# Second block of tokens 0-255 woven with the expert gather of tokens 256-511

## What is computed

```python
def expert_block(args):              # per block of 128 tokens
    hb, eb, gb = args
    a = jax.nn.gelu(jnp.einsum('td,ted->te', hb, u_tab[eb]).astype(jnp.float32), approximate=False)
    w = (gb * a).astype(hb.dtype)
    return jnp.einsum('te,ted->td', w, v_tab[eb])
...
mask = k_chunk[None, :] <= (q_pos // CHUNK)[:, None]
...
```

## Time and profile before

| | us |
|---|---|
| median of 3 runs | 2968.13 (2965.42 to 2969.78) |
| the profiled execution | 2965.35 |
| its span in the profile | 2963.6 |
| first layer and scores, to the start of `stage_peer` | 0 to 677.6 |
| `stage_peer` | 677.6 to 2052.6 |
| half a | 2052.6 to 2467.6 |
| half b | 2467.6 to 2963.6 |

### The profile page before, as it was taken

One profiled execution on the slowest core, in us unless ns is written; L12 is line 12 of the kernel. 1 busy time (PEld: TensorE's weight loads), 2 busy tenths in 40 slices (PEclk: granted clock), 3 DMA queues, 4 the chain that ended last, 5 costly groups with the idle time before them and its releaser, 6 DMA issues. The chain is left out here.

```text
span 2963.6 us, 22217 instructions
## 1 busy us (share of the span) xinstructions
PE 2303.9 (78%) x7379; PEld 1329.2 (45%) x7379; DVE 1289.2 (44%) x2945; ACT 744.4 (25%) x1626; POOL 1071.8 (36%) x746
## 2 busy tenths in 40 slices
PE   4896698681677777777786877776967997778899
PEld 1345343571233333333332333332746885556787
DVE  1107541317667666775668555554252102243101
ACT  1202231211111111111111111112444444344443
POOL 1000000220434444444443444442704885400687
PEclk8897698895898999989998999987958998866999
DMA  6100151323999999999999999995603664300465
GB/s 214 51 14 0 57 171 57 94 74 127 420 420 420 409 420 420 420 385 419 421 419 416 398 420 420 420 420 230 212 0 99 186 185 141 107 1 8 144 185 161
DMA packets 172295, 710.32 MB, mean 240 GB/s; under 512 B 18033, under 2 KB 70812, under 8 KB 106140
## 3 DMA queue, kind: packets, MB, share of 16 engines
q0 software_dynamic: 73728, 536.90, 43.8%
q1 hardware_dynamic: 90576, 168.18, 18.0%
q10 hardware_dynamic: 7886, 3.93, 0.5%
HBM read 699.24 MB, written 9.72 MB: 239 GB/s over the span
## 5 line engine op out<-in xcount | busy, mean ns | idle before, releaser
L1382 PE MATMUL ps<-uv_ring,expert_diag 128*128 128x512 f32 x2048 | 1008.1, 650 | 340.4 <-ACT expert_diag L1351 340.3
L1187 POOL DMA_INDIRECT uv_ring<-in_peer_uv_dram,expert_idx x512 | 556.2, 1086 | 821.5 <-PE ps L1382 712.5
L1306 DVE CUSTOM_DVE_ANT_0 uv_ring<-uv_ring,h_rows 128x1024 f32<-128x1024 f32 x512 | 628.9, 1230 | 492.0 <-DMA uv_ring<-in_peer_uv_dram,expert_idx 491.4
L1382 PEld LDWEIGHTS ps<-uv_ring,expert_diag 128*128 128x128 f32 x2048 | 414.4, 208 | 933.5 <-issue 500.3
L1464 POOL TENSOR_TENSOR w_low_b<-w_raw_b,w_high_b 128x1024 fp32r<-128x1024 f32 x98 | 234.4, 2394 | 262.6 <-ACT w_high_b L1458 261.2
L1351 ACT ACTIVATE expert_diag<-ident,expert_weight 128x128 f32<-128x128 f32 x512 | 163.6, 390 | 623.5 <-DVE expert_weight L1278 623.5
L1464 POOL TENSOR_TENSOR w_low_a<-w_raw_a,w_high_a 128x1024 fp32r<-128x1024 f32 x98 | 235.2, 2403 | 199.4 <-ACT w_high_a L1458 198.1
L271 POOL TENSOR_TENSOR peerq_low<-peerq_raw,peerq_high 128x1024 fp32r<-128x1024 f32 x16 | 38.1, 2381 | 550.6 <-ACT peerq_high L260 550.6
L1344 ACT ACTIVATE expert_gelu<-expert_dot 128x4 f32<-128x4 f32 x128 | 26.3, 205 | 495.7 <-DVE expert_dot L1306 495.7
L1458 ACT CAST w_high_b<-w_raw_b 128x1024 fp32r<-128x1024 f32 x98 | 102.9, 1053 | 116.8 <-PE ps L1477 116.8
L1458 ACT CAST w_high_a<-w_raw_a 128x1024 fp32r<-128x1024 f32 x98 | 102.9, 1052 | 115.4 <-PE ps L1477 115.4
(11 more groups left out here) (399 smaller groups left out, 2896.2 us busy)
## 6 DMA issues: line engine op xcount, KB each, us to landing
w_raw_a<-in_w_gu_dram SPq DMA_DIRECT2D x44, 512.0 KB, 3.5
w_raw_b<-in_w_gu_dram SPq DMA_DIRECT2D x44, 512.0 KB, 3.6
wada_rest<-in_w_ada_dram SPq DMA_DIRECT2D x16, 1024.0 KB, 5.3
w_raw_a<-in_w_in_dram SPq DMA_DIRECT2D x24, 512.0 KB, 4.4
w_raw_b<-in_w_in_dram SPq DMA_DIRECT2D x24, 512.0 KB, 4.0
w_raw_a<-in_w_down_dram SPq DMA_DIRECT2D x22, 512.0 KB, 3.6
w_raw_b<-in_w_down_dram SPq DMA_DIRECT2D x22, 512.0 KB, 3.5
wada<-in_w_ada_dram SPq DMA_DIRECT2D x4, 2048.0 KB, 8.5
```

What stands on the lines that cost most here:

```text
L1187: pool.indirect_dma_start(out=ring[:, n % RING, :], out_offset=None, in_=K.uv, in_offset=bass.IndirectOffsetOnAxis(ap=idx[tb % 2][:, s:s + ...
L1306: dve.tensor_tensor_reduce(u, u, hN[:, tb, :], 1.0, 0.0, ALU.mult, ALU.add, a[tb % 2][:, s:s + 1]).then_inc(s_dot, 1)
L1382: last = nc.tensor.matmul(K.ps[2 * (tb % 2) + half][:, :], diag[n % DIAGS][:, :], ring[:, n % RING, D + 512 * half:D + 512 * half + 512], ...
```

## The change

The gather and the second block are rearranged in three stages:

- `stage_gather` runs blocks 0 and 1 alone (256 slots), with a new class `Gather`: ring of 12, groups of G = 2, 4 diagonals, routing in two halves of 4 heads each (the first 64 indices are ready after the first half). It also routes block 2, and the copies for the attention bias (`BiasRows`) move here.
- half a of the second block (tokens 0-255, tag `_a`) is woven with a second `Gather` for blocks 2 and 3: ring of 6, G = 2, 4 diagonals, `share` = 4: of every four slots the V rows of the last are summed by DVE (one scalar_tensor_tensor 128x1024, `add`) and not by PE. PE has 192 slots, DVE 64. The PSUM banks 6 and 7 are the gather's; `Diff` has one set of score banks and `Ffn` two up-projection banks. `Weights` has 3 raw and 2 split buffers, and cast and subtraction are one tile ahead of the product. The planned step of `Diff` goes from 4.0 to 6.0 and of `Stick` from 1.6 to 3.2; the gather's slots are spread evenly over the plan (`g.us = plan.us / g.n`), which puts 8 slots beside the first norm and transposes, 41 beside In2, 31 beside Diff, 42 beside Stick, 16 beside Out2, 7 beside the second norm, the rest, some 112, beside Ffn.
- half b (tag `_b`) runs alone, as before.

To have the rows of x and h for it, `stage_peer_scores` transposes both back (64 transposes, 16 copies shared by ACT and DVE, 16 stores of 256 KB on ACT's DMA queue) ahead of its first weight cast, and `stage_out1` stores nothing. Each half loads its x rows and bias from DRAM. `dk` of `Diff` lies in two pieces for half b, one matmul more where a score row crosses them. SiLU becomes Tanh on ACT and two scalar_tensor_tensor on DVE, in both halves.

```diff
-            for c in range(2):
-                sp.wait_ge(pr.s_free[c], 1 + 4)
-            sp.dma_start(K.x_dram.rearrange("k p s -> p k s"), K.xres[:, :, :]).then_inc(s_spill, 16)
-            sp.wait_ge(s_spill, 16)
...
+        ROWS = [(src, dst, b, half) for src, dst in ((K.hT, K.h_dram), (K.xres, K.x_rows)) for b in range(TB) for half in range(2)]
...
+            for n, (src, _, b, half) in enumerate(ROWS):
+                if n >= 4:
+                    pe.wait_ge(s_rc[n % 2], (n - 4) // 2 + 1)
+                for k in range(4):
+                    last = nc.tensor.transpose(K.ps[4 + n % 4][:, k * P:(k + 1) * P],
+                                               src[:, 4 * half + k, b * P:(b + 1) * P], K.ident[:, :])
+                last.then_inc(s_rt, 1)
...
             h.high(act)
+            for n, (_, dst, b, half) in enumerate(ROWS):
+                if n % 2 == 0:
+                    act.wait_ge(s_rt, n + 1)
+                    if n >= 4:
+                        act.wait_ge(s_rs[n % 4], 16 * (n // 4))
+                    act.copy(rows[n % 4][:, :], K.ps[4 + n % 4][:, :]).then_inc(s_rc[0], 1)
+                act.wait_ge(s_rc[n % 2], n // 2 + 1)
+                act.dma_start(dst[b, :, 512 * half:512 * half + 512], rows[n % 4][:, :]).then_inc(s_rs[n % 4], 16)
             pr.highs(act, PEER_H, 0)
...
+class Gather:
...
+    G, DIAGS, HG = 2, 4, 4
...
+    def at(self, n):
+        return self.start + self.us * n
+
+    def here(self, n):
+
+        return self.share > 0 and n % self.share == self.share - 1
+
+    def added(self, n):
+
+        own = (n + 1) // self.share if self.share else 0
+        return (self.s_own, own) if self.here(n) else (self.s_pv, n + 1 - own)
...
+    def pool(self, pool):
+        K = self.K
+        for n in range(self.n):
+            b, s = divmod(n, SLOTS)
+            yield self.at(n - self.RING + 2.5)
+            if s % 64 == 0:
+                i = 2 * (b - (1 if self.routed else 0)) + s // 64 + 1
+                if i > 0:
+                    pool.wait_ge(self.s_idx, i)
+            if n == self.RING - 1:
+                pool.wait_ge(self.s_gr, 1)
+            if n >= self.RING:
+                pool.wait_ge(*self.added(n - self.RING))
+            pool.indirect_dma_start(
+                out=self.ring[:, n % self.RING, :], out_offset=None, in_=K.uv,
+                in_offset=bass.IndirectOffsetOnAxis(ap=K.idx[self.blocks[b] % 2][:, s:s + 1], axis=0),
+            ).then_inc(self.s_land[n % self.RING], 16)
...
+        def add(n):
+            b, s = divmod(n, SLOTS)
+            v, x = self.ring[:, n % self.RING, D:2 * D], self.w[:, s:s + 1]
+            dve.wait_ge(self.s_w, n // G + 1)
+            if s < self.share:
+                ins = dve.tensor_scalar(self.acc[:, :], v, x, None, ALU.mult)
+            else:
+                dve.wait_ge(self.s_own, n // self.share)
+                ins = dve.scalar_tensor_tensor(out=self.acc[:, :], in0=v, scalar=x, in1=self.acc[:, :],
+                                               op0=ALU.mult, op1=ALU.add)
+            ins.then_inc(self.s_own, 1)
...
+            dve.wait_ge(self.s_land[n % self.RING], 16 * (n // self.RING + 1))
+            u = self.ring[:, n % self.RING, 0:D]
+            dve.tensor_tensor_reduce(u, u, self.h[b][:, :], 1.0, 0.0, ALU.mult, ALU.add,
+                                     self.a[:, s:s + 1]).then_inc(self.s_dot, 1)
...
+            if n % G == 0 and n:
+                yield place + 0.1 * self.us
+                weigh(n // G - 1)
+                for q in range(n - G, n):
+                    if self.here(q):
+                        add(q)
...
+            yield self.at(G * g + 1.1)
+            act.wait_ge(self.s_dot, G * (g + 1))
+            act.activation(self.gl[:, c], self.a[:, c], ACT.Gelu).then_inc(self.s_gelu, 1)
+            yield self.at(G * g + 2.2)
+            act.wait_ge(self.s_w, g + 1)
+            for j in range(G):
+                if self.here(g * G + j):
+                    continue
+                q = self.added(g * G + j)[1] - 1
+                if q >= self.DIAGS:
+                    act.wait_ge(self.s_pv, q - self.DIAGS + 1)
+                act.activation(self.diag[q % self.DIAGS][:, :], K.ident[:, :], ACT.Copy,
+                               scale=self.w[:, s + j:s + j + 1]).then_inc(self.s_diag, 1)
...
+            yield self.at(n - n % self.G + 2.3 + 0.1 * (n % self.G))
+            if self.here(n):
+                continue
...
+        g = Gather(K, ctx, blocks, False, ahead, 0.0, 2.5, (6, 7), 12)
...
-    KK, RAW, SPLIT, LEAD = 2, 4, 3, 2
-
-    def __init__(self, K, ctx):
+    KK = 2
+
+    def __init__(self, K, ctx, raw, split):
         self.K, self.src, self.at = K, [], []
+        self.RAW, self.SPLIT, self.LEAD = raw, split, split - 1
...
-                ins = mm(nc, self.score(i, c), self.half.dq(h, b)[r, :], self.half.dk(h, self.width(i))[r, :])
+                for c0, keys in self.half.dk(h, self.width(i)):
+                    ins = mm(nc, self.score(i, c)[:, c0:c0 + keys.shape[1]], self.half.dq(h, b)[r, :], keys[r, :])
...
-                    act.activation(self.silu[b][:, :], self.bank(g, b)[:, 0:256], ACT.Silu).then_inc(self.s_silu, 1)
+                    act.activation(self.silu[b][:, :], self.bank(g, b)[:, 0:256], ACT.Tanh, scale=0.5).then_inc(self.s_silu, 1)
...
-                    dve.tensor_tensor(self.prod[b][:, :], self.silu[b][:, :], self.bank(g, b)[:, 256:512],
-                                      ALU.mult).then_inc(self.s_prod, 1)
+                    dve.scalar_tensor_tensor(out=self.silu[b][:, :], in0=self.silu[b][:, :], scalar=1.0,
+                                             in1=self.bank(g, b)[:, 0:256], op0=ALU.add, op1=ALU.mult).then_inc(self.s_gated, 1)
+                    dve.wait_ge(self.s_gated, g * self.nb + b + 1)
+                    dve.scalar_tensor_tensor(out=self.prod[b][:, :], in0=self.silu[b][:, :], scalar=0.5,
+                                             in1=self.bank(g, b)[:, 256:512], op0=ALU.mult, op1=ALU.mult).then_inc(self.s_prod, 1)
...
+    def sp(self, sp):
+        K = self.K
+        yield -30.0
+        for b in range(self.nb):
+            sp.dma_start(self.x[b], K.x_rows[self.b0 + b]).then_inc(self.s_x, 16)
+        sp.dma_start(self.bias[:, :, :], bass.AP(K.b_dram.tensor, 127 + S - self.wb,
+                                                 [[639, P], [P * 640, DIFF_H], [1, self.wb]])).then_inc(self.s_bl, 16)
...
+        g = Gather(K, ctx, experts, True, None, 0.0, 1.0, (6, 7), 6, 4) if experts else None
+        W, plan = Weights(K, ctx, 3 if g else 4, 2 if g else 3), Plan()
...
-        diff = Diff(K, plan, half, p2.done(), (bias.s_bm, 1) if bias else p2.done()[0],
...
+            diff = Diff(K, plan, half, p2.done(), (half.s_bm, 1),
+                        {"s": (0, 1), "t": (2, 3), "o": (4, 5)} if g else {"s": (0, 1, 2, 3), "t": (4, 5), "o": (6, 7)})
...
+        ffn = Ffn(K, W, plan, half, t3, (4, 5) if g else (4, 5, 6, 7), (0, 1, 2, 3))
+        if g:
+            g.us = plan.us / g.n
...
+            weave(*([g.pool(pool)] if g else []), W.lows(pool))
...
+            weave(*([g.act(act)] if g else []), W.highs(act),
...
+def stage_block2(K, ctx):
+
+
+    K.idx = [K.sb(ctx, f"expert_idx{i}", [P, SLOTS], U32) for i in range(2)]
+    K.gate = [K.sb(ctx, f"expert_gate{i}", [P, SLOTS]) for i in range(2)]
+    K.tag = "_g"
+    stage_gather(K, [0, 1], 2)
+    K.recycle()
+    K.tag = "_a"
+    first = Half(K, ctx, 0, 2, None, 6.0, 3.2)
+    stage_half(K, first, [2, 3])
+    K.recycle()
+    K.tag = "_b"
+    stage_half(K, Half(K, ctx, 2, 2, first, 4.0, 1.6), None)
...
```

705 lines of the change are left out of this document (361 added, 344 removed).

## The result

The changed kernel takes 3062.19 us (median of 4 runs, 3050.05 to 3076.74) against 2966.78 (4 runs) of the kernel before on the same chips: ratio 1.032, 95% interval 1.027 to 1.038. The forecast was 2924, with a range of 2810 to 3060.

The account below looks back on a forecast made before the run. DMA was taken to bound the gather, PE mostly the halves, leaving 57% of half a's DMA time unused. Prefix 677.6 + 16, gather 708, woven stage 1013, half b 508 and 1.8 outside the span gave 2924 us, range 2810 to 3060.

Parts of the forecast that it names:

- the 1.1 us per step of Stick: Woven Stick: handovers to DVE and PE add 1.1 us to ACT's 7.2, making 8.3 per step.
- the X of the ring's loop: Woven gather ring: waits behind other work on each engine, 5.5 us per loop beside weight tiles.
- T = 3.9: Woven stage beside weight tiles: 3.9 us per gather slot, 686 us for 176 slots.
- Prefix, +16: peer_scores: transposes, copies and stores ahead of the first weight cast add 16 us, four store rounds of 4.
- stage_gather, 708: Gather of blocks 0 and 1: 38 to stream start, 8 first landing and dot, 648 stream, 14 tail; 708 us.
- DVE's sums buy nothing: Woven stage: DVE summing 64 slots takes 125 us from PE but saves no time, PE not being the floor.
- Start, 40: Woven stage's start: 8 slots beside norm and transposes take 40 us.
- Diff, 100: Woven Diff: 31 slots at 3.2 us, the ring's pace without weight tiles, take 100 us; table loads fit in.
- Stick, 172: Woven Stick: 16 steps of 8.3 us, 133, plus 10 slots around them at 3.9, 39; 172 us.
- Table drain (a rival): Diff and Stick: each of 81 table loads holds ACT twice its 1.28 us, 104 more, total 3028; chance 0.05.
- Port and order (the rival that came out on its side): Woven stage: DVE dots and POOL subtractions hold each other up, T = 4.5 plus 0.15, total 3056; chance 0.29.
- Half b, 508: Half b alone: 496 before, plus x rows from DRAM, queued weight loads and two-piece dk, gives 508 us.

Follow-up runs that it names:

- e10: Changed kernel with ring of 8, blocks 2 and 3 routed in the gather stage, no slots beside Stick, share 2 for 4: 2837.21 us, ratio 0.959.
- e7: Changed kernel with share 0 in place of 4, so PE takes the V rows of all 256 woven slots: 3135.31 us.
- e2: Changed kernel with a woven gather ring of 5 buffers in place of 6: 3188.23 us.
- e5: Changed kernel with a woven ring of 8, blocks 2 and 3 routed in the gather stage, last block's gates not divided by their sum: 3002.95 us.
- e4: Changed kernel in whose woven stage POOL fills each weight tile's low part with zeros instead of subtracting: 3009.46 us.
- e3: Changed kernel with ACT's Copy in place of Gelu in the woven stage, so those table switches go: 3011.43 us.
- e1: Changed kernel with the weave alone undone: all four gather blocks in one stage, then half a and half b alone: 2990.36 us.

## Why the prediction was wrong

The direction was wrong, and the time lies just outside the range. Two steps of the woven stage's sum failed: the 1.1 us per step of Stick for all that its chain waits for, where ACT waits 5.4, and the X of the ring's loop, which gave T = 3.9 where 4.23 to 4.4 was measured. The start (20 us) and Diff (17) add to them. By its own steps:

- **Bound before; free DMA time.** Right: half a leaves it, and e10 takes 137 us of the woven stage's 1063 out of it.
- **Prefix, +16.** Measured 693.5 - 677.6 = 15.9, but the number was lucky. Four rounds of 4 us for the stores don't exist: the 256 KB stores land 2.1 and 2.2 us behind their issue (median), which is also what stores of this size take in the trace of before (`out_dram`, 2.1); the 5.5 of the earlier trace rows was not the only landing on record. What takes the time is ACT's own row of eight copies, each with two DMA issues, 1.53 us a round.
- **stage_gather, 708.** Measured 715, near it by errors of both signs: 64 us to the first dot where 38 + 8 = 46 had been counted, then 639 for the stream (648) and 12 for the tail (14). The DMA share is 0.99 in the stream and 0.94 over the whole stage, not 1.00.
- **DVE's sums buy nothing.** Wrong, and the step that failed is the comparison of PE's 727 us with a stage of 1013: a sum over the stage says nothing of Ffn, where PE is busy 376 of 465 us and stands in its order before ready work for up to 45 more, nor of Stick, where V products lie in the chain. e7 prices it: 73 us for 64 sums, 44 of them in Ffn and 18 in Stick. It has no part in the miss itself, since the forecast was for share 4.
- **T = 3.9 beside weight tiles.** Measured 4.23 to 4.4; with In2, Out2 and Ffn 55 us of the miss. The form of the loop was right (e2, e5 move it the right way), X was too small by some 1.4 us per loop. The port had been given 0.9 per loop, 0.23 per slot; e4 bounds it at 0.43 in Ffn and 0.15 in In2. Which other part of X was too small no run shows.
- **Start, 40.** Measured 60. The x rows were asked for at 1412.4 and used at 1435.8; the first DMAs of the gather and 3.5 MB of other loads had been asked for before them, and the DMA engines are busy 0.95 of the time from 1408 to 1436. The gate rows, which the first dot and the sixth gather DMA wait for, come at 1431.7. The sum had priced neither.
- **Diff, 100.** Measured 117, 3.8 per slot where 3.2 was taken. Neither the tables (e3: 113) nor the port (e4: 118) make much of it; a ring of 8 brings it to 102.
- **Stick, 172.** Measured 234, the largest single error. ACT's 7.2 us per step were right (112 us busy in the 16 steps, 7.0). The 1.1 for the rest of the chain was the failed term: ACT waits 5.4 per step, 3.8 of it for the next scores. Between the diagonals of one step and those scores stand the V products of one slot or, every second time, of two: 3.78 us and 5.2 to 6.5, at a granted clock of 0.50 for the most part, where the kernel before had nothing. e3 shows both: loads 2.9 per step on the path, and 9.0 that stay.
- **Table drain (a rival).** Refuted by the 61 loads from 1759 to 1960 in this trace: each starts 0.02 behind the instruction before it, and in 55 cases the next activation starts 0.01 to 0.02 behind the load (1866.17 + 1.28, next at 1867.47); the other six are gelus, which start 0.8 to 4.6 behind it. The loads cost their 1.28.
- **Port and order (the rival that came out on its side).** The time, 3056, is near the measured one by chance: T was not 4.65, and the rival kept Stick at 172. The port is real, but e4 bounds it at 53 us of a miss of 138; Stick, 62 over its forecast, is the largest single excess.
- **Half b, 508.** Measured 497, the same as before; e1 has 507 at a granted clock of 0.83, this one 0.85, so x and bias from DRAM cost less than what the clock moves. The bias is 1 MB by the trace, not 2.

What stays open: which share of e4's 53 us is the lock and which the shorter instruction on POOL; what in Ffn holds a ring of 8 at 4.09 with share 4; and why share 0 costs 44 us in Ffn and nothing in In2.

## What to carry to other kernels

Before work is woven into idle time of a resource, write down phase by phase, not over the whole stage, each engine's busy time and what it must wait for in its own order. Waits fill up the rest on every engine, so count only those in front of work that is ready, and let a run that takes work away from the engine say whether it counts. A weave through a ring needs enough buffers for the longer loop that it creates; memory for them was found by moving routing into the stage ahead, where DVE was idle. Keep interleaved work out of a chain whose engines pass single results to each other, above all if functions of different ACT tables would alternate there, and count an engine's two-input instructions against those of the engine that shares its port.

## What the runs showed of the hardware that was not expected

- A dot product of two SBUF inputs that starts 0.3 us behind a 2.40 us POOL subtraction takes 3.20 us; up to 3.91 (median 1.22). With POOL writing only (e4), all 256 lie between 1.204 and 1.228.
- A gather DMA's issue on POOL is held by such a dot as well. In the trace of before 134 of 512 issues take over 1.2 us (median 0.94); 123 of them end 0.81 to 0.82 us behind the end of a dot.
- A table load costs its 1.28 us and nothing around it, even with four loads in 10 us.
- The same product takes 1.88 us at a granted clock of 1.00 and 3.78 at 0.50, to which the clock had fallen in Stick, where PE idles 4 to 6 us between its products.
- Two loads of 512 KB (`x_rows_a`) that are issued behind the gather's first DMAs land after 22.5 us (median); the same two in half b (`x_rows_b`), with no gather beside them, after 5.7.
